# Sample heads of a hybrid decoder layer: state reads on two column halves, state updates on two row halves of the matmul array

## What is computed

```
num   = w_inter * (q @ C) + (q k^T * w_intra) @ v        # per sample b and head h
den   = w_inter * (q . n) + sum(s)
h     = num / max(|den|, exp(-m))
C_new = decay * C + sum_s w_end[s] * k[s] v[s]^T
n_new = decay * n + sum_s w_end[s] * k[s]
```

## Time and profile before

| | |
|---|---|
| median of 3 runs | 1964.58 us (1964.14 to 1965.5) |
| the profiled execution | 1967.0 us |
| its span, first to last instruction | 1965.3 us |
| mean granted clock of TensorE | 0.989 of full speed |
| PE busy | 1908.4 us, 97% of the span |
| DVE, ACT, POOL busy | 829.4, 621.2, 128.4 us |
| the sample heads | 757.2 to 935.2 us of the span |

### The profile page before, as it was taken

How to read it: one execution, slowest core, us unless ns; L and a number is a source line. 1 busy time by engine, 2 the same in 40 slices (tenths; PEclk the granted TensorE clock), 3 DMA queues, 4 the chain that set the end, 5 groups by cost and what they waited for, 6 DMA issues and landing times.

```text
span 1965.3 us, 30471 instructions
## 1 busy us (share of the span) xinstructions
PE 1908.4 (97%) x12193; PEld 1815.0 (92%) x12193; DVE 829.4 (42%) x1363; ACT 621.2 (32%) x952; POOL 128.4 (7%) x245
## 2 busy tenths in 40 slices
PE   7999999999999999999999997899999999999998
PEld 4799989999999997777899997899999999999998
DVE  5422222213334333232553558844455545564542
ACT  4331222222434433121210215533333334343432
POOL 0010009201000002221000000000000000000000
PEclk9999999999999999999999998999999999999999
DMA  8653434452343345544642350422232223774641
GB/s 273 239 177 120 132 122 135 140 151 73 93 128 106 92 150 129 165 142 143 203 123 89 90 175 25 109 67 67 71 111 80 65 65 119 261 240 149 214 152 63
DMA packets 254045, 257.70 MB, mean 131 GB/s; under 512 B 15476, under 2 KB 213160, under 8 KB 253952
## 3 DMA queue, kind: packets, MB, share of 16 engines
q1 hardware_dynamic: 244830, 222.81, 37.7%
q10 hardware_dynamic: 7721, 29.25, 3.7%
q0 software_dynamic: 1408, 4.46, 0.8%
HBM read 189.97 MB, written 66.63 MB: 131 GB/s over the span
## 4 chain that ended last, share of the span: by engine, by line
PE 92%; DVE 3%; ACT 2%; DMA 1%; issue 1%; SPq 0%; ACTq 0%; DVEq 0%
PE dense L2340 44%; PE dense L2760 17%; PE dense L2805 10%; PE misc L2760 5%; PE misc L2805 3%; PE misc L2641 2%; PE misc L2628 1%; PE misc L2567 1%; PE misc L2571 1%; PE misc L2540 1%; DMA ada_w<-in_w_ada_dram 1%; PE dense L2414 1%; PE misc L2569 1%; PE misc L2461 1%; PE misc L2460 1%
## 5 line engine op out<-in xcount | busy, mean ns | idle before, releaser
L2340 PE MATMUL dense<-act_hi,w_hi 128*128 128x384 f32 x1704 | 401.2, 343 | 5.8 <-DVE act_lo L1593 3.0
L2340 PE MATMUL dense<-act_lo,w_hi 128*128 128x384 f32 x1704 | 377.4, 329 | 0.0
L2340 PE MATMUL dense<-act_hi,w_lo 128*128 128x384 f32 x1704 | 376.9, 329 | 0.0
L2340 PEld LDWEIGHTS dense<-act_hi,w_hi 128*128 128x128 f32 x1704 | 291.9, 189 | 28.3 <-issue 21.4
L2340 PEld LDWEIGHTS dense<-act_hi,w_lo 128*128 128x128 f32 x1704 | 293.0, 189 | 0.0
L2340 PEld LDWEIGHTS dense<-act_lo,w_hi 128*128 128x128 f32 x1704 | 292.0, 189 | 0.0
L1588 DVE TENSOR_TENSOR w_lo<-raw,w_hi 128x1024 fp32r<-128x1024 f32 x73 | 92.4, 1267 | 265.9 <-ACT w_hi L1028 265.8
L1124 ACT ACTIVATE stage<-dense 128x768 f32<-128x768 f32 x52 | 42.2, 812 | 285.1 <-PE dense L2340 285.0
L1028 ACT ACTIVATE w_hi<-raw 128x1024 fp32r<-128x1024 f32 x73 | 77.3, 1060 | 167.7 <-PE dense L2340 167.3
L2047 DVE TENSOR_TENSOR w_lo<-hmT,w_hi 128x512 fp32r<-128x512 f32 x120 | 78.9, 686 | 101.2 <-ACT w_hi L1334 101.2
L1334 ACT ACTIVATE w_hi<-hmT 128x512 fp32r<-128x512 f32 x120 | 72.6, 623 | 81.2 <-PE dense L2760 80.8
(11 more groups left out here) (435 smaller groups left out, 3051.2 us busy)
## 6 DMA issues: line engine op xcount, KB each, us to landing
z_scratch<-stage ACTq DMA_DIRECT2D x52, 544.0 KB, 2.7
raw<-in_w_in_dram SPq DMA_DIRECT2D x53, 512.0 KB, 3.8
ada_w<-in_w_ada_dram SPq DMA_DIRECT2D x24, 1024.0 KB, 5.5
hmT<-in_w_gate_up_dram SPq DMA_DIRECT2D x40, 512.0 KB, 6.1
raw<-in_w_down_dram SPq DMA_DIRECT2D x34, 512.0 KB, 4.4
stage<-in_w_down_dram SPq DMA_DIRECT2D x32, 512.0 KB, 4.4
stage<-z_scratch SPq DMA_DIRECT2D x24, 544.0 KB, 3.7
a_scratch<-sums SPq DMA_DIRECT2D x34, 272.0 KB, 4.8
```

Source lines behind the costliest of these rows:

```text
L2340: ins = pe.matmul(tile(k, c), w[:, n % 2, off:off + P], x[:, xr, t0:t1], start=(first and p == 0), stop=(last and p == 2))
```

## The change

The two channel halves of a state read go to different column halves of the array: half a=0 writes result partitions 0 to 63, half a=1 partitions 64 to 127, each half adding up over the 8 samples on its own. A new matmul with a stationary matrix `fold` (two identity matrices on top of each other) then adds the two halves into the result of slot 3, in place of the addition on DVE. The updates take two samples together: `kb` and `vs` have the 64 tokens twice, on partitions 0 to 63 for the even sample and on 64 to 127 for the odd one. A slot now serves one half a of two samples. For the doubled tokens, the transposes of slot 0 have a 128-column stationary operand, k and v rows are loaded twice, and `scol` is loaded to both halves of the partitions. POOL makes 4 `kb` blocks of 128 partitions instead of 8 of 64, and a few masks are built later since their memory moved. The order of the sums in the states' rounds follows the new slots.

```diff
-        scol = sb(top, "scol", [SMP, 4, H])
+        scol = sb(top, "scol", [P, 4, H])
...
+        def update_round(b, a):
+            return 4 + 4 * (b // 2) + 2 * a + b % 2
...
                 for h in range(H):
-                    sp.dma_start(scol[:, q, h:h + 1], ...
+                    for p0 in (0, SMP):
+                        sp.dma_start(scol[p0:p0 + SMP, q, h:h + 1], ...
...
             def head_rows(s, h):
-                for g, zr in enumerate((Z_Q, Z_K, Z_V)):
-                    sp.dma_start(qkvs[s][:, 2 * g:2 * g + 2, :],
+                for dst, zr in [(qs_[s][:, :, :], Z_Q)] + [(kv2[s][:, g, :, SMP * d:SMP * d + SMP], (Z_K, Z_V)[g])
+                                                           for g in range(2) for d in range(2)]:
+                    sp.dma_start(dst, ...
...
                 for a in range(2):
-                    wait_full(sp, round_free, R_SMP + RPH * h + 4 + 2 * b + a)
+                    wait_full(sp, round_free, R_SMP + RPH * h + update_round(b, a))
...
+            link(pool.tensor_tensor(fold[:, :], ident[:, 0:SMP], ident[:, SMP:P], ALU.add))
             link(pool.memset(qm[:, :, :, :], 0.0))
...
-                    for b in range(NB):
-                        pool.tensor_scalar(kb[:, b, :], ks[:, :], wmask[:, s, b:b + 1], None, ALU.mult
+                    for b2 in range(NB // 2):
+                        pool.tensor_scalar(kb[:, b2, :], ks[:, :], wmask[:, s, b2:b2 + 1], None, ALU.mult
...
-                    act.activation(hsS[:, :], bank(rb + 2, E1, SMP), ACT.Copy, scale=curC[:, s, 1:2]
+                    act.activation(hsS[:, :], bank(rb + 2, E1), ACT.Copy, scale=curC[:, s, 1:2]
...
-                    wait_full(dve, round_free, rb + 2, i, per)
                     full(3)
-                    dve.tensor_tensor(hnS[:, :], bank(rb + 3, E1, SMP), hsS[:, :], ALU.add
+                    dve.tensor_copy(hnS[:, :], bank(rb + 3, E1, SMP))
...
-                            ins = pe.transpose(misc[0:SMP, (rb + 1) % 2, c0:c0 + P], src[:, a, :], ident[:, :])
+                            ins = pe.transpose(misc[:, (rb + 1) % 2, c0:c0 + P], kv2[s][:, g, a, :], ident[:, :])
...
-                            ins = pe.matmul(bank(rb + 2, E1, SMP), qm[:, b, a, :], cs[s][:, b, a, :],
-                                            start=(b == 0 and a == 0), stop=(b == NB - 1 and a == 1))
+                            ins = pe.matmul(bank(rb + 2, E1)[SMP * a:SMP * a + SMP, :], qm[:, b, a, :], cs[s][:, b, a, :],
+                                            start=(b == 0), stop=(b == NB - 1))
...
-                    give(pe.matmul(bank(rb + 3, E1, SMP), pTS[:, :], vs[:, :], start=True, stop=True), rb + 3)
+                    pe.matmul(bank(rb + 3, E1, SMP), pTS[:, :], vs[0:SMP, :], start=True, stop=False)
+                    wait_full(pe, round_free, rb + 2, i, per)
+                    pe.sem_inc(passed, 1)
+                    give(pe.matmul(bank(rb + 3, E1, SMP), fold[:, :], hsS[:, :], start=False, stop=True), rb + 3)
                 if 4 <= slot < 12:
-                    b = slot - 4
-                    pe.wait_ge(head_kb, h * NB + (b + 1))
-                    for a in range(2):
-                        r = rb + 4 + 2 * b + a
-                        take_s(r)
-                        give(pe.matmul(bank(r, E1), kb[:, b, P * a:P * a + P], vs[:, :], start=True, stop=True), r)
+                    b2, a = (slot - 4) // 2, slot % 2
+                    pe.wait_ge(head_kb, h * (NB // 2) + (b2 + 1))
+                    for odd in range(2):
+                        take_s(rb + update_round(2 * b2 + odd, a))
+                    for odd in range(2):
+                        r, p0 = rb + update_round(2 * b2 + odd, a), SMP * odd
+                        give(pe.matmul(bank(r, E1), kb[p0:p0 + SMP, b2, P * a:P * a + P], vs[p0:p0 + SMP, :],
+                                       start=True, stop=True), r)
```

More of the change, by code:

```diff
@@ L226, in trunk @@
         sb(smp, "rest_qkv1_to_cur", [P, 24])
-        kb = sb(smp, "kb", [SMP, NB, HD])
-        hsS = sb(smp, "hsS", [SMP, E1])
+        kb = sb(smp, "kb", [P, NB // 2, HD])
+        kv21 = sb(smp, "kv21", [P, 2, 2, P])
+        argS = sb(smp, "argS", [SMP, 2, SMP])
+        maskS = sb(smp, "maskS", [SMP, SMP])
+        fold = sb(smp, "fold", [P, SMP])
+        qs1 = sb(smp, "qs1", [P, 2, SMP])
+        curD = sb(smp, "curD", [P, 2, NB])
+        wmask = sb(smp, "wmask", [P, 2, NB // 2])
+        sb(smp, "rest_kb", [P, 104])
+        hsS = sb(smp, "hsS", [P, E1])
         qm = sb(smp, "qm", [P, NB, 2, SMP])
-        ks = sb(smp, "ks", [SMP, HD])
+        ks = sb(smp, "ks", [P, HD])
         sb(smp, "rest_vext_to_hs", [P, 8])
         sb(smp, "over_cst", [P, H * 2 * E1])
-        vs = sb(smp, "vs", [SMP, E1])
+        vs = sb(smp, "vs", [P, E1])
         hnS = sb(smp, "hnS", [SMP, E1])
@@ L239, in trunk @@
         urows = sb(smp, "urows", [HIST + SMP, PW])
-        qkvs1 = sb(smp, "qkvs1", [P, 6, SMP])
         nT = sb(smp, "nT", [P, 2, HC])
[L242 to L249, removed]
+        sb(smp, "rest_hn_hf_sm", [P, 472])
+        qs0 = sb(smp, "qs0", [P, 2, SMP])
+        kv20 = sb(smp, "kv20", [P, 2, 2, P])
+        blk = sb(smp, "blk", [P, NB // 2])
+        curC = sb(smp, "curC", [P, 2, 4])
         smS = sb(smp, "smS", [SMP, 8])
-        cs, qkvs = (cs0, cs1), (qkvs0, qkvs1)
+        cs, qs_, kv2 = (cs0, cs1), (qs0, qs1), (kv20, kv21)
         nout = nrow
@@ L620, in _ @@
                 for h in range(H):
-                    sp.dma_start(scol[:, q, h:h + 1],
-                                 tab_s_dram[q, h * NB:(h + 1) * NB].rearrange("b (t o) -> (b t) o", o=1)
-                                 ).then_inc(tables_in, 16)
+                    for p0 in (0, SMP):
+                        sp.dma_start(scol[p0:p0 + SMP, q, h:h + 1],
+                                     tab_s_dram[q, h * NB:(h + 1) * NB].rearrange("b (t o) -> (b t) o", o=1)
+                                     ).then_inc(tables_in, 16)
             l1_loads(4, 6)
@@ L648, in _ @@
             sp.wait_ge(x_spilled, 16)
-            sp.wait_ge(tables_in, 18 * 16)
+            sp.wait_ge(tables_in, 34 * 16)
             sp.wait_ge(outs, 5 * 16)
@@ L949, in _ @@
             pool.wait_ge(d_out, 2 * PG * 16)
-            pool.wait_ge(tables_in, 18 * 16)
+            pool.wait_ge(tables_in, 34 * 16)
             pool.wait_ge(outs, 5 * 16)
@@ L971, in _ @@
                                      [:, :, ds(ci, 1)].rearrange("p h o -> p (h o)")).then_inc(chunk_prep, 1)
+            link(pool.memset(blk[:, :], 1.0))
+            for p0, first in ((0, 0), (SMP, NT)):
+                m = blk[p0:p0 + SMP, :]
+                link(pool.affine_select(out=m, in_=m, compare_op=ALU.is_ge, fill=0.0,
+                                        base=-first, pattern=[[-2 * NT, NB // 2]], channel_multiplier=1))
+                link(pool.affine_select(out=m, in_=m, compare_op=ALU.is_ge, fill=0.0,
+                                        base=first + NT - 1, pattern=[[2 * NT, NB // 2]], channel_multiplier=-1))
+            for r in (R_UT - 4, R_UT - 3):
+                wait_full(pool, round_free, r)
             link(pool.memset(maskS[:, :], 0.0))
@@ L1001, in _ @@
                                        ).then_inc(head_prep, 1)
-                    pool.wait_ge(head_rows_in[s], i * (3 * 16) + 3 * 16)
+                    pool.wait_ge(head_rows_in[s], i * (5 * 16) + 5 * 16)
                     pool.sem_inc(passed, 1)
                     for b in range(NB):
-                        pool.tensor_copy(qm[:, b, :, NT * b:NT * b + NT], qkvs[s][:, 0:2, NT * b:NT * b + NT]
+                        pool.tensor_copy(qm[:, b, :, NT * b:NT * b + NT], qs_[s][:, :, NT * b:NT * b + NT]
                                          ).then_inc(head_prep, 1)
@@ L1265, in _ @@
                     act.wait_ge(head_prep, h * 11 + 11)
-                    act.activation(wexpS[:, s, :], argS[:, s, :], ACT.Exp, bias=curC[:, s, 0:1]).then_inc(weights_exp, 1)
+                    act.activation(wexpS[:, s, :], argS[:, s, :], ACT.Exp, bias=curC[0:SMP, s, 0:1]).then_inc(weights_exp, 1)
                     wait_full(act, round_full, rb + 2, i, 2 * RPH)
-                    act.activation(hsS[:, :], bank(rb + 2, E1, SMP), ACT.Copy, scale=curC[:, s, 1:2]
+                    act.activation(hsS[:, :], bank(rb + 2, E1), ACT.Copy, scale=curC[:, s, 1:2]
                                    ).then_inc(round_free[(rb + 2) % 2], 1)
@@ L1861, in _ @@
                     full(1)
-                    dve.tensor_copy(ks[:, :], bank(rb + 1, HD, SMP)).then_inc(head_keys, 1)
-                    dve.tensor_copy(vs[:, 0:HD], bank(rb + 1, 512, SMP)[:, HD:512]).then_inc(round_free[(rb + 1) % 2], 1)
+                    dve.tensor_copy(ks[:, :], bank(rb + 1, HD)).then_inc(head_keys, 1)
+                    dve.tensor_copy(vs[:, 0:HD], bank(rb + 1)[:, HD:512]).then_inc(round_free[(rb + 1) % 2], 1)
                     split_lo(U_GM + 2 * s + 1, i, 4)
```

(24 more changed lines are left out.)

5 lines of the change are left out of this document (2 added, 3 removed).

## The result

The changed kernel takes **1940.45 us** (median of 4, 1938.56 to 1941.45) against 1965.04 us before in the same comparison: a ratio of 0.9872, with an interval of 0.9857 to 0.9888. That is 24.6 us less, where 13.7 were forecast. The profiled execution took 1941.45 us, with a span of 1939.7.

What follows compares the result with a forecast made beforehand. PE was taken as the bound, with 92% of the chain of waits; -9.1 (reads) - 6.9 (updates) + 2.3 (fold) + 0.05 (slot 0) = -13.7 us, median 1950.9 us, own range 1947.9 to 1954.2, wider 1946.5 to 1961.

Steps and rivals of the forecast that it cites:

- the forecast's own range: Whole-kernel median with both forms overlapping, from all loads hidden to all exposed: 1947.9 to 1954.2 us, chance 0.67.
- the wider one: Whole-kernel range from 1946.5 us, the best end less 1.4 between runs, to 1961: chance 0.80.
- 4u becomes 3u: Update slots: with u = 0.217 us instruction spacing, only the first of B overlaps the second of A; 6.9 us at most.
- Reads: Eight read stretches of 16 instructions, two column halves partly overlapping, B's load exposed at changes of half: -9.1 us.
- the row chosen as nearest: Read stream, [rows 6]: load and preceding matmul both stand at 762.47; that order taken for B's load, giving -9.1 us.
- Updates: 32 update slots on two row halves, loads taken as hidden: -6.9 us; 3.6 saved if exposed, 0 without overlap.
- Fold: Slot 3: one more matmul per head, with a gap for changed shape and its load, 0.56 x 4 = +2.3 us.
- Slot 0: Transposes: first load has 128 columns, +0.05 us for head 0; heads 1 to 3 hide it in idle time that stays.
- Covers on SP, POOL, ACT and DVE: Other engines' added or moved work, such as table loads, `kb` blocks and late masks, stays hidden from PE: costed at nothing.
- One form only: Rival: only reads overlap, 1957.8 to 1954.8 us, chance 0.08; or only updates, 1960.0 or 1963.3, chance 0.10.
- No overlap: Rival: reads and updates keep 16u and 4u; changes of half free, 1966.9 us, chance 0.06, or paid, 1980.0, 0.09.
- the paid one: Rival: no overlap, and 88 changes of half in reads and updates cost 13.0 us: 1980.0, slower, chance 0.09.

Runs made afterwards that it cites:

- reads alone: Changed kernel with each update slot back to one sample's two channel halves, reads still on two column halves: 1954.87 us, 0.9933 of the kernel before.
- updates alone: Changed kernel with reads back in one 64-row result and DVE's addition instead of the fold: 1951.86 us, 0.9919 of the kernel before.

## Why the prediction was wrong

The sign, the place and the mechanism were right: PE bounds the heads, two halves of the array run side by side, and what is saved there leaves the total. How far they run side by side was wrong: two terms were too small, and the forecast's own range and the wider one both ended above the result.

**The step that failed** is the sentence "Each half needs its own two instructions in turn, but the first of B can run beside the second of A", and with it "4u becomes 3u". By it the next matmul, though of the other half, could begin no earlier than with the last instruction of the pair ahead. The 7 ns between the starts of both halves' firsts show that nothing of the kind holds: the halves run their pairs beside each other.

- *Reads*: said -9.1, with -12.2 for "the upper end"; measured 64u, 13.9 us. Loads were to be exposed at 7 changes of half per stretch; none is, and the row chosen as nearest for this, one load beginning with the matmul before it, was a row of one and the same half.
- *Updates*: said -6.9, and that was the end too; measured 13.6 to 13.9. No choice within the bounds could have saved this term: the end itself was wrong. The bound that the step should have had needs no idea of the order at all: n instructions on two places take at least n/2 starts, 8u and 2u.
- *Fold*: said +2.3 (4 times 0.56 is 2.24); 770.50 - 769.92 = 0.58 per head, 2.3.
- *Slot 0*: said +0.05; the four transposes are recorded as 0.66 instead of 0.63, and the idle times of heads 1 to 3 stayed as said.
- *Covers on SP, POOL, ACT and DVE*: held, as the rows show.

With the measured terms the sum is -13.9 - 13.9 + 2.3 = -25.5 for 25.3 in the heads; the two mis-sized terms, 4.8 and 7.0, make up all of the 11.8 us between the 1953.3 forecast for the profiled execution and its 1941.45.

The rivals fell. "One form only" is refuted by reads alone and updates alone, each of which shortens its own slot by all that sharing can give. "No overlap", free or paid, is refuted by the timeline. Of the paid one, its price was put at 0.13 to 0.18 us per change of half; what shows is 7 ns, while the change of shape before the fold did cost its 0.09.

One sentence of the Trainium skill, "TensorE: Matmul & The Clock Gate", Part 3, The mechanism, lets a load overlap running matmuls only where their row groups differ; the same section also names a load into the background weight buffer, which the prediction left out. The reads disagree with the one sentence: both halves use all 128 rows, and their loads and matmuls start 7 ns apart. The updates of reads alone show the other side: two halves of the channels on the same 64 rows and on all 128 columns kept 1.13, so what counts is that the parts of the array differ, by rows or by columns. The Trainium skill, "TensorEngine Tiling (Array Packing)", Key Properties, says that different tiles load and multiply in parallel, and that only a change of mode drains the engine. The traces agree on the first: 8u, 2u and 4u for two and four parts. On the second they show 7 ns for a change of half and a gap of 0.09 us for the change of shape at the fold; whether the engine drains in it they do not show.

## What to carry to other kernels

Where PE is the bound and a float32 matmul fills only a half or a quarter of the array, give the rest to a second one, and bound the gain by the count of instructions over the count of parts. Alternate the parts in program order; with two parts, two in a row per part cost only an unhidden load of 0.05 us per stretch, four in a row 4u. Let neighbouring small matmuls have equal shapes and go in and out of another stream as seldom as can be, and put a part that waits for another engine one block later.

## What the runs showed of the hardware that was not expected

- A part's first matmul starts 7 ns behind the other's, and a 32-bit matmul's two instructions don't hold up another part.
- Four parts of 32 columns on the same 128 rows run at once: 16 instructions in 4u.
- Half 1 was held for 4u behind four matmuls of half 0 and for nothing behind two: order counts. One running and one waiting per part is one account of it, three instructions yet to start in all is another, and the runs leave both standing.
- Not every change of the recorded shape has a gap. From the last transpose to the next dense matmul it is 28 ns before, where the transposes have 64 stationary columns and the dense matmul 128, and 29 ns now, where both have 128 (759.612 to 759.640 and 760.500 to 760.529 in the single records). What sets the gap of 0.09 at the fold apart is not shown.
- Four row quarters for the updates were not tried: they need four results open at once, and there are two banks for them here.
